# Head norms in the differential-attention stage: exact fp32 sums against two rounded products of split squares

## The reference, cut to what matters

```
q, k, v = jnp.split(jnp.einsum('btd,de->bte', h, w_in), [nqk, 2 * nqk], axis=-1)
q = rms_norm(q.reshape(B, T, DIFF_HEADS, 2, DIFF_HD), q_gain)   # x * rsqrt(mean(x*x over 64) + eps) * gain
k = rms_norm(k.reshape(B, T, DIFF_HEADS, 2, DIFF_HD), k_gain)
```

## Time and profile before

| what | value |
|---|---|
| median of 3 runs | 1408.65 us (1408.03 to 1409.03) |
| the profiled execution | 1407.64 us, its span 1405.7 us |
| TensorE matmul busy | 1377.0 us, 98% |
| weight loads busy | 1297.7 us, 92% |
| VectorE, ScalarE busy | 950.9 us (68%), 654.9 us (47%) |
| GpSimd busy | 89.2 us (6%) |
| granted TensorE clock, mean | 0.998 of full speed |
| chain that ended last | PE 89%, DVE 4%, ACT 3%, issue 2%, DMA 1% |

### The profile page before, as it was taken

The page is one execution under the profiler, slowest core; times in us unless marked ns, Lnnn a source line. Parts: engine busy times, 40 slices in busy tenths (PEclk is TensorE's granted clock), DMA queues, the critical chain, the costliest instruction groups (busy, mean ns, idle before and its releaser), DMA issues.

```text
span 1405.7 us, 26326 instructions
## 1 busy us (share of the span) xinstructions
PE 1377.0 (98%) x10896; PEld 1297.7 (92%) x10896; DVE 950.9 (68%) x1592; ACT 654.9 (47%) x1456; POOL 89.2 (6%) x149
## 2 busy tenths in 40 slices
PE   8999999999999999999999999999999999999999
PEld 6878888999999999999888787889899999999999
DVE  4588786579988788678765646566888654554554
ACT  4543344365553354351565555653665552552430
POOL 0000000210000000000300000000300000000000
PEclk9999999999999999999999999999999999999999
DMA  9644543244444543534423223112344222223222
GB/s 380 225 156 147 180 147 98 68 153 148 165 143 158 180 158 129 194 114 151 178 107 105 102 99 136 62 57 69 117 135 140 86 79 102 90 68 114 76 67 105
DMA packets 37582, 182.42 MB, mean 130 GB/s; under 512 B 4246, under 2 KB 6422, under 8 KB 26072
## 3 DMA queue, kind: packets, MB, share of 16 engines
q1 hardware_dynamic: 22552, 126.98, 25.9%
q0 software_dynamic: 14912, 53.78, 11.0%
HBM read 172.82 MB, written 7.91 MB: 129 GB/s over the span
## 4 chain that ended last, share of the span: by engine, by line
PE 89%; DVE 4%; ACT 3%; issue 2%; DMA 1%; POOL 0%; SPq 0%; DVEq 0%; POOLq 0%; ACTq 0%
PE ps L644 26%; PE ps L646 26%; PE ps L645 26%; DVE sq L1679 1%; PE ps L1030 1%; DVE h_lo L1692 1%; PE ps L1071 1%; DMA a_pro<-in_ada_w 1%; PE ps L989 1%; PE ps L1049 1%; ACT w_hi L1129 1%; PE ps L882 1%; PE ps L878 1%; PE ps L682 1%; PE ps L869 1%
## 5 line engine op out<-in xcount | busy, mean ns | idle before, releaser
L646 PE MATMUL ps<-h_hi,w_lo 128*128 128x272 f32 x2080 | 601.6, 289 | 0.0
L644 PE MATMUL ps<-h_hi,w_hi 128*128 128x272 f32 x1984 | 578.8, 292 | 5.3 <-ACT up L1403 1.7
L645 PE MATMUL ps<-h_lo,w_hi 128*128 128x272 f32 x1984 | 570.6, 288 | 0.0
L646 PEld LDWEIGHTS ps<-h_hi,w_lo 128*128 128x128 f32 x2080 | 391.0, 188 | 0.0
L644 PEld LDWEIGHTS ps<-h_hi,w_hi 128*128 128x128 f32 x1984 | 373.4, 188 | 16.7 <-issue 7.3
L645 PEld LDWEIGHTS ps<-h_lo,w_hi 128*128 128x128 f32 x1984 | 373.9, 188 | 1.0 <-issue 1.0
L1129 ACT CAST w_hi<-w_raw 128x2048 fp32r<-128x2048 f32 (+2 forms) x108 | 182.9, 1695 | 196.8 <-PE ps L646 169.1
L1605 DVE TENSOR_TENSOR w_lo<-w_raw,w_hi 128x2048 fp32r<-128x2048 f32 (+2 forms) x107 | 219.7, 2053 | 69.2 <-ACT w_hi L1129 68.6
L645 PE MATMUL ps<-act_lo,w_hi 128*128 128x272 f32 (+1 forms) x704 | 203.8, 290 | 0.0
L644 PE MATMUL ps<-act_hi,w_hi 128*128 128x272 f32 (+1 forms) x704 | 203.5, 289 | 0.0
L646 PE MATMUL ps<-act_hi,w_lo 128*128 128x272 f32 (+1 forms) x704 | 203.2, 289 | 0.0
(11 more groups left out here) (266 smaller groups left out, 1734.8 us busy)
## 6 DMA issues: line engine op xcount, KB each, us to landing
w_raw<-in_wst SPq DMA_DIRECT2D x73, 1024.0 KB, 4.9
a_raw<-in_ada_r POOLq DMA_DIRECT2D x56, 512.5 KB, 4.6
w_raw<-in_wst SPq DMA_DIRECT2D x28, 768.0 KB, 4.3
a_raw<-in_ada_g POOLq DMA_DIRECT2D x24, 512.0 KB, 3.6
a_pro<-in_ada_w SPq DMA_DIRECT2D x8, 1024.0 KB, 18.5
v_raw<-in_wst SPq DMA_DIRECT2D x8, 1024.0 KB, 8.1
w_raw<-in_wst SPq DMA_DIRECT2D x8, 512.0 KB, 3.8
xT<-in_xT SPq DMA_DIRECT2D x4, 544.0 KB, 6.9
```

Of the source, the lines that this page charges most:

```text
L644: mm(out, lhs_hi, rhs_hi, start=first, stop=False)
L645: mm(out, lhs_hi, rhs_lo, start=False, stop=False)
L646: return mm(out, lhs_lo, rhs_hi, start=False, stop=last)
```

## The change

For pairs 1 to 3 each 512-column head sum becomes two fp32r matmuls with the rounded constant `bones_r`: one on the squares' high part `sq_hi`, one on the low part `sq_low`. ACT makes the high part by a copy behind the evacuation of the second half of each tile, and waits first for its own evacuation and for the head sum that read `sq_hi` last. DVE makes the low part by a subtraction that waits for the copy. `sq_low` takes the memory of `sq`, and `sqq_low` that of `sqq`. The two sample sums stay fp32, and so do all six of pair 0. Five of the six sums of a pair get another place: idx 1 from first to second slot of position 4, idx 2 from the second slot of 4 to the first of 5, idx 3 from first to second of 5, idx 4 from first to second of 6, idx 5 from the second of 6 to the second of 7; idx 0 stays. DVE makes `bones_r` once, just ahead of the differential stage. The space in SBUF for GpSimd's transfer descriptors is halved, from 8192 to 4096.

```diff
-NORM_FIRST = {4: [1], 5: [3], 6: [4]}
-NORM_THEN = {3: [0], 4: [2], 6: [5]}
+NORM_FIRST = {5: [2]}
+NORM_THEN = {3: [0], 4: [1], 5: [3], 6: [4], 7: [5]}
...
-        sq = sb("sq", [P, 2, T])
+        whole = ExitStack()
+        sq = sb("sq", [P, 2, T], c=whole)
+        whole.close()
+        sq_low = sb("sq_low", [P, 2, T], F32R)
...
+        sqq_low = sb("sqq_low", [P, 2, T], F32R, c=d)
+        sq_hi = sb("sq_hi", [P, 2, TP], F32R, c=d)
+        bones_r = sb("bones_r", [P, P], F32R, c=d)
...
-                mm(ps[:, head_bank(p, idx), 0:TP if piece < 2 else 2 * TS], bones, rhs, start=True, stop=True).then_inc(hsum_ok, 1)
+                if p and piece < 2:
+                    if n == 6:
+                        pe.wait_ge(bones_ok, 1)
+                    pe.wait_ge(sq_low_ok, 4 * (p - 1) + 2 * which + piece + 1)
+                    out = ps[:, head_bank(p, idx), 0:TP]
+                    mm(out, bones_r[:, :], sq_hi[:, piece, :], start=True, stop=False)
+                    mm(out, bones_r[:, :], (sq_low, sqq_low)[which][:, piece, 0:TP], start=False, stop=True).then_inc(hsum_ok, 1)
+                else:
+                    rhs = src[:, piece, 0:TP] if piece < 2 else src[:, :, TP:T]
+                    mm(ps[:, head_bank(p, idx), 0:TP if piece < 2 else 2 * TS], bones, rhs, start=True, stop=True).then_inc(hsum_ok, 1)
...
                     A_(dst[:, p % 2, t, s], ps[:, b, 0:HALF], ACT.Identity, scale=gain_).then_inc(evac_a, 1)
+                    if half == 1 and p:
+                        act.wait_ge(evac_a, U_EVAC[u])
+                        if kind == "dq" or p > 1:
+                            act.wait_ge(hsum_ok, 6 * p + t + 1 - (0 if kind == "dq" else 3))
+                        act.copy(sq_hi[:, t, :], squares[:, t, 0:TP]).then_inc(sq_hi_ok, 1)
...
+                if kind in ("dk", "dq") and half == 1 and BL[n][1]:
+                    which, p = int(kind == "dq"), BL[n][1]
+                    dve.wait_ge(sq_hi_ok, 4 * (p - 1) + 2 * which + t + 1)
+                    TT((sq_low, sqq_low)[which][:, t, 0:TP], (sq, sqq)[which][:, t, 0:TP], f32(sq_hi[:, t, :]), ALU.subtract).then_inc(sq_low_ok, 1)
...
+            dve.tensor_copy(bones_r[:, :], bones).then_inc(bones_ok, 1)
...
-    nc = bacc.Bacc("TRN2", target_bir_lowering=False, num_devices=1, dynamic_dma_scratch_size=8192)
+    nc = bacc.Bacc("TRN2", target_bir_lowering=False, num_devices=1, dynamic_dma_scratch_size=4096)
```

More of the change, by code:

```diff
@@ L381, in hybrid_stream_step @@
         qT = sb("qT", [P, 2, 2, T], c=d)
-        sqq = sb("sqq", [P, 2, T], c=d)
+        dq_whole = ExitStack()
+        sqq = sb("sqq", [P, 2, T], c=dq_whole)
+        dq_whole.close()
+        sqq_low = sb("sqq_low", [P, 2, T], F32R, c=d)
+        sq_hi = sb("sq_hi", [P, 2, TP], F32R, c=d)
+        bones_r = sb("bones_r", [P, P], F32R, c=d)
         vd = sb("vd", [P, 2, NR, BC], c=d)
@@ L460, in hybrid_stream_step @@
         lam_ok, lam_exp, lam_done = sem("lam_ok"), sem("lam_exp"), sem("lam_done")
+        bones_ok, sq_hi_ok, sq_low_ok = sem("bones_ok"), sem("sq_hi_ok"), sem("sq_low_ok")
         hsum_ok, hlog_ok, hinv_ok, heads_ok = (sem(x) for x in ("hsum_ok", "hlog_ok", "hinv_ok", "heads_ok"))
@@ L987, in head_sums @@
                         pe.wait_ge(od_out, 3 * (p - 1))
-                rhs = src[:, piece, 0:TP] if piece < 2 else src[:, :, TP:T]
-                mm(ps[:, head_bank(p, idx), 0:TP if piece < 2 else 2 * TS], bones, rhs, start=True, stop=True).then_inc(hsum_ok, 1)
+                if p and piece < 2:
[8 more added lines that the diff above has]
+                    mm(ps[:, head_bank(p, idx), 0:TP if piece < 2 else 2 * TS], bones, rhs, start=True, stop=True).then_inc(hsum_ok, 1)
             def turn_heads(p, part, bank):
```

## The result

| | kernel before | changed kernel |
|---|---|---|
| median | 1408.03 us (1407.48 to 1409.03, 5 runs) | 1419.81 us (1417.88 to 1425.77, 5 runs) |
| ratio | | 1.0085 (95% interval 1.0069 to 1.0100) |
| profiled execution, its span | 1407.64, 1405.7 us | 1425.77, 1423.8 us |
| mean granted TensorE clock | 0.998 | 0.987 in the profiled execution, 0.992 to 0.994 in the others |

The change costs 11.8 us, twice the 6.0 that were forecast, and the time is 2.0 us above the range's upper end. Slower was right, the size was not. The last row of the table is what the forecast did not have: the clock.

A forecast was written before the change was run, and what follows sets the result against it. TensorE carries the chain but waits for ACT's full list in positions 6 to 8; 1.9 us per pair gives +5.8 over three preparations, plus 0.2 for `bones`: +6.0, 1414.6 us against the median, range 1410.5 to 1417.8.

The forecast's parts named there:

- What bounds, and the chain on ACT: TensorE waits for ACT's full list between position 5's unit and position 6's `turn_weights`; anything added there adds time, instruction by instruction.
- Positions 3 to 5: Idx 0 and 1 gain 0.41 us each; position 5's unit ends 1.46 earlier, with 0.2 of new waiting.
- Positions 6 to 8: Late norms of idx 4 and 5: `values_out` 0.57 us later at position 7, 0.6 more waiting at 8; pair 1.9 late.
- Position 5 to 6: ACT's copy (0.65 us) and idx 3's Ln and Exp (1.27) lengthen 3.53; position 6's `turn_weights` starts 0.46 later than before.
- Position 6. Idx 4 now stands behind the unit and costs 0.45: Idx 4's sum costs 0.45 us it didn't before, idx 5 leaves (-0.16); `values` of position 6 is 0.75 late.
- Rival C: More loss: slack of 0.45 us fails in positions 2 and 3, `values` waits for DVE; 1417.8 us, chance 0.07.
- The sum at full clock: The whole forecast: 1.9 us late per pair, +5.8 for three preparations, +0.2 for `bones`, +6.0 in all.
- the +0.2 for `bones_r`: DVE's copy of `bones` stands in a chain on which TensorE waits: +0.2 us, bounds 0 and 0.3.
- Costed at nothing: Subtractions and copies at positions 2 to 4, and the halved descriptor space, were each priced at nothing.
- Rival B: TensorE's own work decides, ACT's list doesn't: 12 times 0.41 us come off, 1403.7 us, faster; chance 0.08.
- Rival D: Old waits at positions 7 and 8 absorb 1.17 of 1.9 us per pair: 1411.1 us, no change; chance 0.09.
- rival E: The 512-column fp32r product is no faster than fp32: 3.7 us more in all, 1418.3 us; chance 0.02.

The follow-up runs named there:

- `norm_behind`: Changed kernel with Ln and Exp of idx 3 moved on ACT alone from ahead of position 5's `values_out` to behind it: 1415.15 us, ratio 1.0040.
- `late_split`: Changed kernel with ACT's rounding of the weight block moved from ahead of position 5's `values_out` to behind it: 1412.90 us, ratio 1.0029.
- `order_alone`: Kernel before with the new places of the sums alone (fp32 products, no rounding copies, no subtractions): 1421.26 us, ratio 1.0088.
- `filled_three`: Changed kernel with needless products in three waits per pair, ahead of `turn_weights` of positions 6 and 7 and `values` of 8: 1413.38 us, ratio 1.0041.
- `filled_wait`: Changed kernel with 14 needless rounded products ahead of position 6's `turn_weights` in each of three preparations: 1415.54 us, ratio 1.0050.
- `space_4096`: Kernel before with the descriptor space alone halved to 4096: 1409.10 us, ratio 1.0002.
- `split_alone`: Changed kernel with the old places of the sums; rounded products, copies and subtractions stay: 1408.90 us, ratio 1.0006.
- `both_repaired`: Changed kernel with the weight block rounded behind position 5's `values_out` and idx 1 to 5 in other places: 1401.81 us, ratio 0.9949 to the kernel before.

## Why the prediction was right or wrong

**What bounds, and the chain on ACT: right.** The step from position 5 to 6 was forecast at 3.53 + 1.92 us and measured at 5.42, the copy takes 0.67 in the list (783.85 - 782.81, less the 843.35 - 842.98 of the earlier trace rows), the two products at 0.46. `norm_behind`, `late_split` and `order_alone` move this wait by what they move on ACT and TensorE.

**Positions 3 to 5: right.** Counted from the first `values` of the stage, `filled_three` starts position 4's `values` 1.0 us earlier than the kernel before (32.37 against 33.33), as forecast, and position 6's `turn_weights` 0.3 later (43.65 against 43.33), where 0.46 was forecast.

**Positions 6 to 8: right.** Forecast 0.57 more at position 7 (1.05 - 0.48 measured), and a longer wait for DVE's copy at position 8, 0.4 more (1.07 - 0.69). A pair at full clock is 1.8 to 1.95 us longer; 1.9 was the forecast.

**The step that failed** is the price of the wait in "Position 5 to 6", and with it the sum. It put `turn_weights` at 841.02 + 3.53 + 1.92 and then went on with "Position 6. Idx 4 now stands behind the unit and costs 0.45", the unit itself taken at its length in the trace of before. Those rows are of a stage whose clock stood at 1.00, with no wait over 1.0 us; the clock is in no term, no bound and no rival. The forecast made a wait of 3.5 us and didn't ask whether the rows behind it would still hold. They did not: the unit behind it steps by 0.213 us where the row said about 0.12. The waits of positions 7 and 8, forecast in their length, were taken as free of such a cost too, and `filled_wait` shows that they weren't: with the long wait filled, the clock still fell behind the last wait of two pairs out of three (1.07 and 1.08 us). The missing term measured 10.1 us in one comparison and about 7 in the other. Rival C named more loss but with another mechanism, DVE late in positions 2 and 3, and there TensorE shows no such wait: the three waits for L2105 are those of position 8.

**The sum at full clock**, +6.0, measured 4.8 by the medians and 5.5 by the trace (`filled_three`). Within it the +0.2 for `bones_r` was nothing: the wait of the earlier trace rows, 0.69 us before, is 0.67 in the first trace of the changed kernel and 0.68 in the second. The direction was no luck, since the steps hold one by one.

**Costed at nothing**: the descriptor space (`space_4096`) and, in the changed kernel's places, the subtractions and copies of positions 2 to 4, where TensorE shows no wait over 0.3 us in the first trace of the changed kernel. With idx 1 in its old place TensorE does idle 0.3 us ahead of it (`split_alone`).

**Rival B** (the 4.9 us of TensorE's work) fell for the reason given against it: `split_alone` gained 0.13 us in a pair. In `both_repaired`, with ACT's stretch shorter by the weight block and the sums in the remaining waits, the product's gain appears. **Rival D** fell because the old waits grew instead of absorbing the lateness, **rival E** because the two products take 0.46 us.

## What to carry to other kernels

Before moving a step by one slot, list what each engine then has between the last result that its neighbour waits for and that neighbour's next work: a 1.3 us norm that sat in idle time became 1.3 us of the chain. And when a change makes a wait on TensorE of more than the trace of before contains, price what runs behind it at both clock levels, because rows taken at the full clock don't hold there. The cheapest test is to fill the wait with needless products; if the kernel gets faster by doing more, the clock is a part of the loss.

## What the runs showed of the hardware that I had not expected

In the first pair of `order_alone` TensorE idled 2.43 us, in that of `norm_behind` 2.24 us, and both stages had a mean clock below 1.00:

```profile
720.00:935.00 215.00, 199.69 (x1515) 169.78 (x1513) 114.25 (x243) 116.53 (x330) 9.77 (x17) 0.97 0.27 92
```

```profile
720.00:935.00 215.00, 200.48 (x1560) 173.41 (x1559) 126.01 (x265) 127.15 (x352) 9.76 (x17) 0.98 0.27 94
```

So the clock fell behind waits much shorter than the changed kernel's 3.49 us, and in `filled_wait` behind waits of 1.07 and 1.08. But it doesn't fall every time: behind the 2.25 us wait of `norm_behind`'s second pair it stayed at 1.00 (849 to 853 us), and the kernel before, with waits of 0.99, 0.48 and 0.69 in a pair, kept 1.00 through the stage. In `split_alone` it fell once, just behind waits of 1.02 and 0.99 us in the first pair, and not behind the waits of the other two pairs, 1.02 and 0.99, 1.02 and 0.56. No run here shows where the limit lies. So runs of one kernel that differ in their mean clock as well as in their time (1417.88 us at 0.994, 1425.77 at 0.987) are a sign to look at the clock in the trace, stage by stage.
